# Modulation vectors as row sums of transposed weights, and a reordered beginning, in a decoder layer on one core

## The reference, cut to what matters

```
c_act = silu(c)
mod = (c_act @ w_ada + b_ada).reshape(3, 3, 1024)       # shift, scale, gate for each sub-layer
h = rms_norm(x, gain) * (1 + scale) + shift
x = x + 0.5 * gate * ((silu(h @ w_g) * (h @ w_u)) @ w_out)      # ffn; the mixer has its own body
```

## Time and profile before

| what | value |
|---|---|
| median of 3 runs | 1157.53 us (1157.37 to 1157.53) |
| span of the profiled execution | 1153.6 us |
| time of the profiled execution itself | not listed apart from its span |
| PE busy | 1071.8 us, 93% |
| DVE busy | 591.5 us, 51% |
| ACT busy | 366.1 us, 32% |
| POOL busy | 101.9 us, 9% |
| read from HBM | 133.50 MB |

### The profile page before, as it was taken

The page is one execution under the profiler, slowest core; times in us unless marked ns, Lnnn a source line. Parts: engine busy times, 40 slices in busy tenths (PEclk is TensorE's granted clock), DMA queues, the critical chain, the costliest instruction groups (busy, mean ns, idle before and its releaser), DMA issues.

```text
span 1153.6 us, 13435 instructions
## 1 busy us (share of the span) xinstructions
PE 1071.8 (93%) x4874; PEld 879.9 (76%) x4874; DVE 591.5 (51%) x748; ACT 366.1 (32%) x475; POOL 101.9 (9%) x78
## 2 busy tenths in 40 slices
PE   0289999999999997997999999988999999999998
PEld 0168888888887886976788888776888888888886
DVE  4976676766654537366755545536333333332221
ACT  2233233232322224256544443424322322321110
POOL 3110000000000001084100002311000000000000
PEclk9999999999999998998999999998999999999999
DMA  9426556555455321222111112221232232222222
GB/s 355 159 73 214 185 183 201 174 203 171 163 173 170 139 98 35 105 87 76 71 38 73 73 68 77 91 92 62 84 109 78 103 109 76 94 76 100 94 82 96
DMA packets 36937, 135.93 MB, mean 118 GB/s; under 512 B 4272, under 2 KB 4528, under 8 KB 28464
## 3 DMA queue, kind: packets, MB, share of 16 engines
q1 hardware_dynamic: 36480, 135.50, 33.8%
q10 hardware_dynamic: 432, 0.11, 0.0%
HBM read 133.50 MB, written 2.10 MB: 118 GB/s over the span
## 4 chain that ended last, share of the span: by engine, by line
PE 83%; DVE 7%; POOL 3%; ACT 3%; issue 2%; DMA 1%; SPq 0%; DVEq 0%; ACTq 0%; POOLq 0%
PE bank L408 26%; PE bank L410 26%; PE bank L409 26%; PE bank L603 2%; DMA ada_first<-w_ada 1%; DVE w_lo L978 1%; DVE first_acc L1010 1%; ACT w_hi L694 1%; POOL window L1524 1%; DVE scaled L1086 1%; DVE ada_acc L1010 1%; DVE h L1094 1%; PE bank L618 1%; POOL window L1529 1%; PE bank L591 1%
## 5 line engine op out<-in xcount | busy, mean ns | idle before, releaser
L408 PE MATMUL bank<-h_hi,w_hi 128*128 128x512 f32 x928 | 365.8, 394 | 12.5 <-DVE h_lo L1100 8.5
L410 PE MATMUL bank<-h_lo,w_hi 128*128 128x512 f32 x928 | 362.9, 391 | 0.0
L409 PE MATMUL bank<-h_hi,w_lo 128*128 128x512 f32 x928 | 362.9, 391 | 0.0
L978 DVE TENSOR_TENSOR w_lo<-w_raw,w_hi 128x2048 fp32r<-128x2048 f32 (+2 forms) x99 | 206.5, 2086 | 145.4 <-ACT w_hi L694 145.4
L408 PEld LDWEIGHTS bank<-h_hi,w_hi 128*128 128x128 f32 x928 | 175.3, 189 | 55.7 <-issue 12.7
L694 ACT ACTIVATE w_hi<-w_raw 128x2048 fp32r<-128x2048 f32 (+3 forms) x100 | 172.2, 1722 | 123.8 <-PE bank L410 63.7
L410 PEld LDWEIGHTS bank<-h_lo,w_hi 128*128 128x128 f32 x928 | 175.2, 189 | 37.0
L409 PEld LDWEIGHTS bank<-h_hi,w_lo 128*128 128x128 f32 x928 | 175.4, 189 | 35.9
L408 PE MATMUL bank<-act_hi,w_hi 128*128 128x512 f32 x352 | 139.3, 396 | 0.0
L410 PE MATMUL bank<-act_lo,w_hi 128*128 128x512 f32 x352 | 139.2, 396 | 0.0
L409 PE MATMUL bank<-act_hi,w_lo 128*128 128x512 f32 x352 | 139.2, 396 | 0.0
(11 more groups left out here) (188 smaller groups left out, 1006.8 us busy)
## 6 DMA issues: line engine op xcount, KB each, us to landing
w_raw<-w_ffn_in SPq DMA_DIRECT2D x44, 1024.0 KB, 5.0
ada_raw<-w_ada SPq DMA_DIRECT2D x112, 256.0 KB, 2.9
w_raw<-w_ffn_out SPq DMA_DIRECT2D x32, 704.0 KB, 4.1
w_raw<-w_mix SPq DMA_DIRECT2D x21, 1024.0 KB, 4.8
ada_first<-w_ada SPq DMA_DIRECT2D x8, 1024.0 KB, 15.9
x<-x_t SPq DMA_DIRECT2D x1, 2048.0 KB, 12.9
out<-x SPq DMA_DIRECT2D x8, 256.0 KB, 3.7
w_raw<-w_mix SPq DMA_DIRECT2D x1, 832.0 KB, 4.3
```

The costliest lines, as they stand in the source:

```text
L408: nc.tensor.matmul(dst, a_hi, b_hi, start=start, stop=False)
L409: nc.tensor.matmul(dst, a_lo, b_hi, start=False, stop=False)
L410: return nc.tensor.matmul(dst, a_hi, b_lo, start=False, stop=stop)
L978: nc.vector.tensor_tensor(w_lo[slot][:, 0:size], w_raw[slot][:, 0:size], w_hi[slot][:, 0:size].bitcast(F32), ALU.subtract).then_inc(lo_don ...
```

## The change

1. **Row sums.** w_ada is laid out transposed on the host, as 72 tiles of 128 output columns x 1024 inputs. c lies in all partitions (`c_wide`, 512 KiB, a DMA of its own, silu on ACT). One DVE instruction (`tensor_tensor_reduce`) multiplies a tile by `c_wide`, sums each row, starts from b_ada and writes one column of `mod`. Accumulators, their splits, the reduction on PE, the diagonal and the bias addition are gone.
2. **The first shift vectors on PE.** For k tiles 0 to 4 the shift tile stays untransposed, and PE multiplies it with c_act in 8 matmuls of one output column (`first_shift_on_pe`); DVE adds the bias.
3. **The beginning k tile by k tile.** DMA order: c_wide, x in four parts, then scale and shift tile of k = 0, weight chunk 0, k = 1 and 2, weight chunk 1, k = 3 to 7. DVE makes modulation and h of one k tile before it goes to the next. PE works on chunks 0 and 1 together (`first_up`).
4. **Sum of squares on PE.** ACT squares x in four parts, PE sums them in 32 one-column matmuls, DVE adds the four partial sums.
5. **h with one instruction fewer.** The gain moves into the first instruction, h's low part is made on DVE from `scaled`, shift and high part, for all k tiles, in all three norms. POOL no longer takes part in it, nor in the first sum of squares or the first weight chunk.
6. **In the first ffn**, `up` has two row sums per chunk, `down` one per chunk in its first 12; the SP and DVE loops of f = 0 are written out, and the two raw buffers for modulation hold 512 KiB each.

The core of the diff:

```diff
+            sp.dma_start(c_wide[:, :], c_rows).then_inc(c_in, 16)
+            for q in range(4):
+                sp.dma_start(x[:, 2 * q:2 * q + 2, :], x_t[:, 2 * q:2 * q + 2, :]).then_inc(x_in[q], 16)
+            first_ada(0)
             load_w(w_ffn_in[0, 0], 0, IN_ELEMS, None)
+            first_ada(1)
+            first_ada(2)
             load_w(w_ffn_in[0, 1], 1, IN_ELEMS, None)
+            for k in range(3, KD):
+                first_ada(k)
...
+            def first_shift_on_pe(k):
+                pe.wait_ge(first_in[2 * k + 1], 16)
+                if k >= 2:
+                    pe.wait_ge(first_shift, k - 1)
+                for kt in range(KD):
+                    last = nc.tensor.matmul(ADA_BANKS[k % 2][:, 0:1], ada_first[:, 2 * k + 1, kt * P:(kt + 1) * P],
+                                            c_act[:, kt:kt + 1], start=kt == 0, stop=kt == KD - 1)
+                last.then_inc(first_shift_sum, 1)
...
+                    first_shift_on_pe(1)
+                    part(0, 0)
+                    first_shift_on_pe(2)
+                    part(0, 1)
+                    first_shift_on_pe(3)
+                    part(0, 2)
+                    for k in range(3):
+                        part(1, k)
+                    first_shift_on_pe(4)
+                    for k in range(3, KD):
+                        part(0, k)
+                        part(1, k)
...
+            def mod_tile(dst, raw, col, done):
+                nc.vector.tensor_tensor_reduce(out=raw, in0=raw, in1=c_wide[:, :], scale=1.0,
+                                               scalar=bias_ada[:, col:col + 1], op0=ALU.mult, op1=ALU.add,
+                                               accum_out=dst).then_inc(done, 1)
...
+            def scale_in(l, m):
+                if m >= 2:
+                    dve.wait_ge(h_ready, KD * l + m - 1)
+                nc.vector.scalar_tensor_tensor(out=scaled[:, m % 2, :], in0=x[:, m, :], scalar=gain_mod[:, m:m + 1],
+                                               in1=bank[4][:, :], op0=ALU.mult, op1=ALU.mult)\
+                    .then_inc(scaled_ready, 1)
+            def low_in(l, m):
+                dve.wait_ge(scaled_ready, KD * l + m + 1)
+                dve.wait_ge(h_hi_ready, KD * l + m + 1)
+                nc.vector.scalar_tensor_tensor(out=h_lo[:, m, :], in0=scaled[:, m % 2, :],
+                                               scalar=mod[:, 3 * KD * l + m:3 * KD * l + m + 1],
+                                               in1=h_hi[:, m, :].bitcast(F32), op0=ALU.add, op1=ALU.subtract)\
+                    .then_inc(h_ready, 1)
...
+            def first_modulated():
+                first_scale_tile(0)
+                first_shift_tile(0)
+                first_gain_col(0)
+                dve.wait_ge(rstd_wide, 1)
+                scale_in(0, 0)
+                half_low(0).then_inc(half_lo_done, 1)
+                low_in(0, 0)
+                half_low(1).then_inc(half_lo_done, 1)
+                for k in range(1, KD):
+                    first_scale_tile(k)
+                    first_shift_tile(k)
+                    first_gain_col(k)
+                    scale_in(0, k)
+                    if k == 2:
+                        dve.wait_ge(half_lo_done, 2)
+                        nc.vector.memset(newton[:, :], 0.0).then_inc(lo_done, 1)
+                        split(1, 1, IN_ELEMS)
+                    low_in(0, k)
```

More of the change, by code:

```diff
@@ L449, in ffn, with up_part @@
                 n0 = FIRST_CHUNK[f]
+                def up_part(s, k):
+                    for gu in range(2):
+                        last = product(bank[2 * s + gu][:, :], w_tile(s, gu * KD + k),
+                                       (h_hi[:, k, :], h_lo[:, k, :]), k == 0, k == KD - 1)
+                    return last
                 def up(i, first):
@@ L729, in norm_high @@
                     nc.scalar.activation(h_hi[:, m, :], scaled[:, m % 2, :], ACT.Identity,
-                                         scale=gain_mod[:, m:m + 1], bias=mod[:, shift + m:shift + m + 1])\
-                        .then_inc(h_hi_ready, 1)
+                                         bias=mod[:, shift + m:shift + m + 1]).then_inc(h_hi_ready, 1)
+                    if l == 0 and m == 1:
+                        split(0, 1, IN_ELEMS)
             def mix_split(k):
@@ L899, in up @@
                         j = 2 * i + s
[L900 to L901 removed]
+                        if not (first and f == 0 and s == 0):
+                            split((n0 + s + 1) // 2 + i, 1 - s, OUT_ELEMS if last and s else IN_ELEMS,
+                                  (pe_used, u0 + j))
                         act.wait_ge(pe_used, u0 + j + 1)
@@ L929, in down @@
                                 square_x(m, m)
-                        if f == 0 and s == 3 and not last:
-                            ada_high(ADA_START + NFH + i)
                 with act.Fori(0, 3) as i:
@@ L1378, in up @@
                         j = 2 * i + s
-                        split(n0 + j + 1, 1 - s, OUT_ELEMS if last and s else IN_ELEMS)
+                        if not (f == 0 and first and s == 0):
+                            split(n0 + j + 1, 1 - s, OUT_ELEMS if last and s else IN_ELEMS)
                         if f == 0:
-                            add_ada(ADA_START + i, range(4 * s, 4 * s + 4))
+                            add_ada(ADA_START + 2 * j)
+                            add_ada(ADA_START + 2 * j + 1)
                         if not (f == 0 and first and s == 0):
@@ L1420, in down @@
                                                            op0=ALU.mult, op1=ALU.add).then_inc(out_evac, 1)
-                        if f == 0 and s == 3 and not last:
-                            ada_low(ADA_START + NFH + i + 1)
-                with dve.Fori(0, 3) as i:
-                    down(i, False)
+                if f == 0:
+                    for i in range(3):
+                        down(i, False)
+                else:
+                    with dve.Fori(0, 3) as i:
+                        down(i, False)
                 down(3, True)
```

379 lines of the change are left out of this document (142 added, 237 removed).

## The result

| | kernel before | changed kernel |
|---|---|---|
| median (4 runs each) | 1157.45 us | 1141.44 us (1138.76 to 1143.61) |
| ratio | | 0.9868, 95% interval 0.9855 to 0.9881 |
| span of the profiled execution | 1153.6 | 1141.8 (its own time 1143.61) |
| PE busy / DVE busy / POOL busy | 1071.8 / 591.5 / 101.9 | 1095.0 / 523.7 / 71.5 |

The change gains 16.0 us where 22.0 were forecast (1135.5); the time lies in the forecast's range. A second measurement of the same kernel gave 1142.36, ratio 0.9876 (0.9860 to 0.9891).

The account below looks back on a forecast made before the run. Chunk 2's start, bound by DMA and DVE, then PE's matmul count and later-norm gaps set the time. -16.2 + 2.1 - 6.4 - 1.7 = -22.2 from span 1153.6 gives 1131.4, plus 3.9: 1135.5 rounded; eight in ten 1127 to 1148.

Parts of the forecast that it names:

- The row sum: One DVE row sum of a 128 x 1024 modulation tile takes 1.28 us; lower end 1.2, upper end 2.44.
- half rate: First rival: DVE row sums at half rate, 2.3 us each, delaying the beginning, for 1146.3 us; chance 0.19.
- The 28 matmuls: First ffn: 14 groups of 2 matmuls of 128x512 leave PE, all on the path, gaining 6.4 us.
- The clock's price: PE's idle gap of 5.1 us before chunk 2 lowers the clock; ten slow matmuls lose 2.1 us, lower end 0.
- The path behind the last k tile: From h's last low part at 63.0, through row sums, product and chunk 2's split, to chunk 2's start at 71.0.
- Tile pitch of the norms: Later norms: each tile takes scaled 0.66 plus low part 0.78, 1.44 us against 1.72 before.
- The mis-sized term: the beginning: Everything up to chunk 2's first matmul: it starts at 71.0 instead of 87.2, gaining 16.2 us.
- The bound of 2 us either way: First norm at startup: allowance of 2 us either way within the forecast's own range of 1129 to 1142.
- k = 4: Fifth k tile of the first norm: waits for PE's 24 matmuls and shift sum until 44.4, ready at 47.1.
- The later norms: Second and third norm: shorter tile pitch gains 0.3 and 1.4 us, together 1.7.
- Low rate through the beginning: Second rival: PE stays at the 1.2 GHz level through the beginning, costing 4.5 us, for 1140; chance 0.11.
- DVE as the bound of up: Third rival: row sums above 2.65 us each make DVE bound up; at 3.3 the time is 1184; chance 0.04.

Follow-up runs that it names:

- the twenty put back: Changed kernel plus 20 extra 128x512 matmuls in the first ffn's up half, two in each chunk of pairs 1 to 10: 1146.38 us, ratio 0.9910.
- the filled gap: Changed kernel plus 24 matmuls with unread results between chunk 1's last matmul and chunk 2's first, where PE stood idle: 1140.91 us, ratio 0.9858.

## Why the prediction was right, and where its sum was not

**Right as it stood.** The row sum: 1.28 forecast, 1.28 measured; two f32 sources with an accumulator took 1280 ns for 1024 columns, with 0.08 us for reading the accumulator beside it. The half rate of some 2.3 us, weighed by the rule of the Trainium skill (Vector Engine (DVE) Microarchitecture Reference, § Points that are easy to get wrong), does not show. The rule is about scalar-tensor-tensor instructions, and the row sum is a custom one in the profile. Those that bear the name are no slower with two f32 sources in SBUF (L1033, 748 ns) than with one of them in PSUM (L1025, 747), but they use no accumulator, so no run here tests the rule itself. The 28 matmuls: 6.4 forecast, 6.3 by the twenty put back. The clock's price: 2.1 forecast, 1.8 in chunk 2's first nine matmuls (0.43 instead of 0.227), 2.0 by the filled gap. The path behind the last k tile: 8.0 forecast (63.0 to 71.0), 8.0 measured. Tile pitch of the norms: 1.44 and 1.44. PE waits for DVE nowhere in the first ffn behind chunk 2's start.

**The mis-sized term: the beginning.** The last low part of h ended at 73.37, not 63.0, and that is the whole miss of the span. The bound of 2 us either way that I gave the norm was missed fourfold (1/rms spread at 30.6, not 22.5). Step by step (forecast, measured, difference):

| step | forecast | measured | |
|---|---|---|---|
| first square done | 10.05 | 11.5 | +1.4 |
| PE's sums of squares | 8.2 | 13.8 | +5.7 |
| from there to the first product | 4.4 | 5.5 | +1.1 |
| first product to low part of k = 3 | 17.1 | 17.6 | +0.5 |
| k = 4 | 7.4 | 9.9 | +2.5 |
| k = 5 to 7 | 15.9 | 15.0 | -0.9 |
| sum | | | +10.3 |

The failing step is the sentence "PE needs 2.04 us for 8 one-column matmuls". The row reads x8, and I took it for eight matmuls of the code, as the section on the kernel before also says. The loop of `norm` makes four; each is two PE instructions. (Read rightly, the row would have given 16.3 for 32, somewhat above the 13.8 measured.) The earlier trace rows held the evidence twice: L446 is a single matmul in the code and is counted x2. The same error sits in the shift vector ("1.0 for the shift's eight", 1.84 measured at the high rate and 3.41 at the low one), and through it in k = 4's wait and in the 1.1 us by which 1/rms was late. The first +1.4 is the last small DMA, landed at 10.2 instead of 9.0.

**Smaller terms.** The later norms: 1.7 forecast; the marks give 1.2 in the third, and 0.3 lost in the second, where a longer stretch at 1.2 GHz followed. The four terms as measured, -5.8 + 1.8 - 6.3 - 0.9, make -11.2 of the -11.8; 0.6 stays unaccounted.

**What was luck.** On the spans the miss is 10.4 us (1131.4 forecast, 1141.8 measured), and the median is off by 5.9 only. The time around the span was 1.8, not the 3.9 that I took from a profile and a median of different executions, which hid 2.1, and the profiled execution after is 2.2 above its median. With 3.9 around the measured span the time would be 1145.7, inside the range for eight in ten but outside the narrower one of 1129 to 1142.

**The rivals.** Half rate: false, and worth 10.3 at chunk 2 when put in by force. Low rate through the beginning: in part true. I had 11 of 24 catching-up matmuls slow, there were 12, and eight more at granted clock 0.51 from 64.8 on; those had cover behind DVE. DVE as the bound of up: false, and its point of decision looks right: a doubled row sum is 2.53 us from start to start, and the 0.32 left for two puts the bound at 2.69 as an estimate; the forecast said 2.65.

**What of the change helped.** Removing the 28 matmuls gave 6.3, by the twenty put back. The rest is the earlier chunk 2 and the third norm; no run separates the row sums from the order k tile by k tile in it. Parts of the same change took from it: the sum of squares on PE 7.1 or more, the shift vectors on PE some 2 to 2.5.

## What to carry to other kernels

Before a duration per instruction is multiplied, divide the profile's count by the number of calls in the code: one f32 matmul was two instructions, and a sum of small matmuls was priced at half. Work moved to an engine "that has time" must be looked at for what stands behind it in the same queue: PE had time in the beginning, yet its one-column matmuls were the path of the norm. When a kernel changes pace in a stage that an edit does not touch, compare the addresses too; here they are the one difference found, and the cause is open. And a gain is read between marks of the two traces: here 2 us came and went in a stretch that no edit touched, and a median has them in it.

## Unexpected of the hardware

- A one-column f32 matmul costs 0.43 us at the low rate (13.79 for 32, 3.41 for 8) and 0.23 at the high one (1.84 for 8), though it moves a single column.
- The first rise of PE's rate does not show in the granted clock: 13 matmuls in 5.2 us and 13 in 2.8, both at 1.00. It came at 51 us in the changed kernel and at about 37 in the one with doubled row sums in the ffn, which has the same instructions up to there, with some tiles 32 bytes further on (as has the kernel with all of them doubled, where it came at 51). Over the experiments it lies between 37 and 51 and does not follow PE's first matmul: that came at 8.2 and the rise at 39.5 in one kernel, at 16.4 and 37 in another.
- 32 bytes in the place of the moving operand went with 3% of PE's pace (259 against 266 matmuls in 60 us); the address was not changed by itself.
- The moment of return to 2.4 GHz behind the second norm, 13 to 16 us after the same update of x, went with 2 us of time in the stretch (337.04 and 338.99), though not in every kernel (16.4 and 337.65 with all row sums on DVE).
